# Second layer's attention: softmax inverses spread by transposes of a wide copy, and one near-score product less for block 0

## The reference

```python
for g, (window, dil) in enumerate(((128, 1), (512, 4), (2048, 16))):
    o, l = dilated_prompt(q_p[:, :, g], kv_p[:, :, g, 0], kv_p[:, :, g, 1], window, dil)
    outs_p.append(o)
    lses_p.append(l)
xp = xp + combine_groups(outs_p, lses_p).reshape(b, s, -1) @ w_o_b[j]
```

## Time and profile before

| | |
|---|---|
| median of 3 runs | 1336.86 us (1336.71 to 1337.3) |
| span of the profiled execution | 1336.2 us |
| PE busy | 1256.2 us, 94% |
| DVE busy | 631.5 us, 47% |
| POOL busy | 494.6 us, 37% |
| layer 1's attention (`layer_b`, main loop) | about 648 to 1029 us of the span |
| experts of layer 1 | from about 1061 us to the end |

### The profile page before, as it was taken

One profiled execution on the slowest core, in us unless ns is written; L12 is line 12 of the kernel. 1 busy time (PEld: TensorE's weight loads), 2 busy tenths in 40 slices (PEclk: granted clock), 3 DMA queues, 4 the chain that ended last, 5 costly groups with the idle time before them and its releaser, 6 DMA issues. The chain is left out here.

```text
span 1336.2 us, 21731 instructions
## 1 busy us (share of the span) xinstructions
PE 1256.2 (94%) x8924; PEld 885.1 (66%) x8924; DVE 631.5 (47%) x1023; ACT 399.9 (30%) x839; POOL 494.6 (37%) x415
## 2 busy tenths in 40 slices
PE   8999998999999998889999999999998999998787
PEld 6787887545666655446969868879746656664443
DVE  3578774623722221155357748638546562221114
ACT  2222322402122221255325425426015312221122
POOL 4466655101111111012986676686640101111101
PEclk9999999999999999989999999999999999999999
DMA  8446644477799999981111112013140999999997
GB/s 315 143 143 222 213 126 171 157 308 307 286 418 419 419 417 419 419 349 48 51 57 57 60 57 97 12 57 99 29 123 13 354 375 417 419 419 419 419 419 293
DMA packets 92102, 318.89 MB, mean 239 GB/s; under 512 B 32297, under 2 KB 44729, under 8 KB 65892
## 3 DMA queue, kind: packets, MB, share of 16 engines
q1 hardware_dynamic: 77284, 279.95, 54.1%
q0 software_dynamic: 13536, 33.29, 7.0%
q10 hardware_dynamic: 1184, 4.26, 0.8%
HBM read 300.19 MB, written 33.28 MB: 250 GB/s over the span
## 5 line engine op out<-in xcount | busy, mean ns | idle before, releaser
L1214 PE MATMUL ps<-slots,oT 128*64 128x256 f32 x1216 | 158.9, 392 | 18.5 <-DMA slots<-in_w_up 17.0
L1214 PEld LDWEIGHTS ps<-slots,oT 128*64 128x64 f32 x1216 | 107.8, 141 | 63.5 <-issue 21.6
L1240 DVE TENSOR_TENSOR sg<-sg,ps 64x256 f32<-64x256 f32 x64 | 26.4, 413 | 240.0 <-ACT sg L1237 240.0
L1726 POOL DMA_INDIRECT xs<-xn_rows,idx x30 | 30.8, 1027 | 236.3 <-PE ps L1203 165.9
L2106 PE MATMUL ps<-slots 128*128 128x384 f32 x320 | 107.4, 490 | 1.5 <-DVE vo L2493 1.5
L1237 ACT ACTIVATE sg<-ps 64x256 f32<-64x256 f32 x64 | 24.4, 382 | 234.1 <-PE ps L1214 234.1
L1732 POOL DMA_INDIRECT y_rows<-ysb,idx x30 | 30.2, 1008 | 168.4 <-DVE ysb L1249 168.4
L2106 PEld LDWEIGHTS ps<-slots 128*128 128x128 f32 x320 | 67.3, 215 | 34.7 <-issue 3.8
L1249 DVE COPY ysb<-ps 64x512 f32<-64x512 f32 x60 | 41.6, 694 | 85.8 <-PE ps L1232 81.8
L1232 PE MATMUL ps<-slots,hT 128*64 128x512 f32 x320 | 74.2, 598 | 4.4 <-issue 4.2
L2430 ACT ACTIVATE slots<-slots,neg 128x128 f32<-128x128 f32 (+1 forms) x192 | 64.3, 421 | 43.3 <-DVE neg L2596 43.3
(11 more groups left out here) (374 smaller groups left out, 2636.1 us busy)
## 6 DMA issues: line engine op xcount, KB each, us to landing
slots<-in_w_up SPq DMA_DIRECT2D x42, 1024.0 KB, 29.3
slots<-in_w_down SPq DMA_DIRECT2D x40, 1024.0 KB, 29.0
slots<-in_w_gate SPq DMA_DIRECT2D x34, 1024.0 KB, 29.0
slots<-in_unit_weights_b SPq DMA_DIRECT2D x12, 1536.0 KB, 6.9
wA<-in_qkv_pairs_a SPq DMA_DIRECT2D x24, 512.0 KB, 3.5
apart<-in_w_gate SPq DMA_DIRECT2D x10, 1024.0 KB, 28.5
spare<-in_w_gate SPq DMA_DIRECT2D x8, 1024.0 KB, 12.3
scratch<-in_w_gate SPq DMA_DIRECT2D x8, 1024.0 KB, 20.0
```

The source lines that it names most:

```text
L1214: last = nc.tensor.matmul(bank(q)[lo:lo + CAP, 0:FE], x[:, k, :], wt[:, k, :], start=(k == 0), stop=(k == KT - 1))
```

## The change

It has two parts.

1. `invert` writes the inverses out on DVE into a new SBUF tile `shares` (128 partitions, 4 blocks by 2 heads by 64 equal values, 512 elements) after the reciprocal, and PE's `spread_inverse` is 4 transposes of 128x128 in place of 8 matmuls. DVE waits for its own reciprocal, and, ahead of the reciprocal, for the spread before.
2. For block 0 of the near group the product with the missing block before it is left out: `scores` of half 0 has one product fewer per head (128 columns), the mask pass is 2x384 elements in place of 2x512, the unused quarter of the score tile is set once to -1e30 by a memset, and the mask table is 640 columns in place of 1024.

```diff
-                      ("m0", 4 * 256), ("m1", 128), ("m2", 128)):
+                      ("m0", 128 + 2 * 256), ("m1", 128), ("m2", 128)):
...
+                shares = sb("shares", [128, 4, 2, HD], to=ph)
...
                         elif half == 0:
-                            for kb in range(2):
-                                for h in range(2):
-                                    product(h, 0, 0, 128 * kb, 128)
+                            for h in range(2):
+                                product(h, 0, 0, 128, 128)
                             for h in range(2):
                                 last = product(h, 1, 0, 256, 256)
...
                         for b in range(4):
-                            for h in range(2):
-                                last = nc.tensor.matmul(bank(3)[64 * h:64 * h + 64, 128 * b:128 * b + 128],
-                                                        inverse[:, pair, b, h:h + 1].to_broadcast([128, HD]), ident, start=True, stop=True)
+                            last = nc.tensor.transpose(bank(3)[:, 128 * b:128 * b + 128], shares[:, b].rearrange("p h e -> p (h e)"), ident)
                         last.then_inc(s_ib, 1)
...
-            V.scalar_tensor_tensor(out=dst.rearrange("p h b k -> p h (b k)"), in0=bank(4, 2).rearrange("p (h x) -> p h x", h=2),
-                                   scalar=SCALE, in1=mask("m0")[:, 512 * half:512 * half + 512].unsqueeze(1).to_broadcast([128, 2, 512]),
+            lo = 0 if half else 128
+            V.scalar_tensor_tensor(out=dst.rearrange("p h b k -> p h (b k)")[:, :, lo:512],
+                                   in0=bank(4, 2).rearrange("p (h x) -> p h x", h=2)[:, :, lo:512], scalar=SCALE,
+                                   in1=mask("m0")[:, 128 * half:128 * half + 512 - lo].unsqueeze(1).to_broadcast([128, 2, 512 - lo]),
...
                         dve_do(V.reduce_sum(inverse[:, pair], total[:, pair].rearrange("p i b h -> p b h i"), AX_X))
-                        V.reciprocal(inverse[:, pair], inverse[:, pair]).then_inc(s_inv, 1)
+                        if 2 * j + pair:
+                            dve.wait_ge(s_ib, 2 * j + pair)
+                        dve_do(V.reciprocal(inverse[:, pair], inverse[:, pair]))
+                        V.tensor_copy(shares.rearrange("p b h e -> p (b h) e"),
+                                      inverse[:, pair].rearrange("p b h -> p (b h)").unsqueeze(2).to_broadcast([128, 8, HD])).then_inc(s_inv, 1)
...
                     dve_do(V.memset(tok[:, :, 4, :], 0.0))
+                    dve_do(V.memset(sc[0][:, :, 0, 0:128], NEG))
```

More of the change, by code:

```diff
@@ L87, in constants @@
     put("sid", np.concatenate([token, token + TOK], 1) - NOROW)
[L88 to L93, removed]
+    own, past = np.where(m <= p, 0, NEG), np.where(m >= p, 0, NEG)
+    put("m0", np.concatenate([own, past, own, past, own], 1))
     put("m1", np.where(m <= p, 0, NEG))
```

## The result

The changed kernel takes 1341.08 us (median of 13 runs), the kernel before 1336.24 (13 runs on the same chip). The ratio is 1.0040, 95% interval 1.0030 to 1.0049: 5.3 us slower, between 4.0 and 6.5 (the means lie 5.3 apart, the medians 4.8). The forecast was 2.8 slower, 1339.7, and the range ended at 1341.3.

What follows compares the result with a forecast made beforehand. PE and DVE were both taken to be at their limit at pair 0's spread, so DVE delays there count in full. +6.6 + 0.1 - 0.1 - 1.6 - 2.2 = +2.8 us on 1336.86 gave 1339.7; range 1334.3 to 1341.3.

Steps and rivals of the forecast that it cites:

- the copy of pair 0: DVE copy after the reciprocal, j = 0 to 2: held by POOL's square, 2.2 us late each time, +6.6 us.
- -1.6: Pair 1's spread on PE in j = 0, 1, 2: transposes save 0.53 us each, 3 x 0.53 us gained.
- -2.2: Product left out of `scores` of half 0: 0.27 us saved in each of 8 steps, on PE or the mask pass.
- The last spread: PE's 1.17 us wait for the reciprocal grows about 0.45 by the copy, transposes give back 0.53: -0.1 us.
- sum of +2.8: Total of all terms over the changed loop: +6.6 + 0.1 - 0.1 - 1.6 - 2.2 us, 0.21% slower.
- rival D: Stalls cost more than themselves: PE idles some 3 us per j, clock or POOL/DVE order suffers; 1342.7 us, chance 0.05.
- from 1000 to 1030 PE idled 3.4 us and the clock stayed 1.00: Profile row around the attention's end, cited as evidence that PE's new stalls would not lower the clock.
- one microsecond per stall: Extra cost assumed for each of PE's stalls in j = 0, 1, 2 if the clock or order suffers, giving 1342.7 us.
- I carry each shift of the attention's end to the end of the program one to one: Behind the attention: experts' weights load only once it ends, so the rest moves as a block.
- +0.1: Pair 0's copy in j = 3, free at +0.46 us on DVE, mostly taken up by PE's earlier transposes.
- B: Rival: pair 0's copy is not held, costing +1.4 (0.42 us) to +2.1 (0.7 us); 1334.5 to 1335.5 us, chance 0.16.
- C: Rival: DVE has hidden room before `p_copy(j, 7)`, PE alone sets the pace; -6.4 us, 1330.5 us, chance 0.07.

Runs made afterwards that it cites:

- r5: Changed kernel with pair 0 spread by the old matmuls without copy, pair 1 still by copy and transposes: 1331.88 us, 0.9970 of the kernel before.
- r6: Changed kernel with the copy to `shares` replaced by a reduction over an axis of length one: 1338.07 us, 1.0009 of the kernel before.
- r7: Changed kernel with POOL's square made to wait until pair 0's copy is done: 1335.72 us, 0.9988 of the kernel before.
- r2: Kernel before with only the second part of the change (product left out, shorter mask pass, narrow table), old spread: 1332.55 us, 0.9969 of before.
- r1_again: The changed kernel measured again with no edit: 1342.06 us, 1.0044 of the kernel before.
- r8: Changed kernel with unread filler products in PE's waits in the stages of j = 0 to 2: 1342.30 us, 1.0041 of the kernel before.
- r9: Changed kernel with unread filler products in the stages of j = 0 to 2 and ahead of the last spread: 1338.71 us, 1.0015 of before.
- r12: Repeat of the changed kernel with pair 0 on the old matmuls and only pair 1 on copy and transposes: 1334.73 us, 0.9982 of before.
- r10_again: The changed kernel measured once more with no edit, sent last: 1342.74 us, 1.0043 of the kernel before.
- r11: Changed kernel with two unread filler products only ahead of the last spread: 1343.57 us, 1.0048 of the kernel before.
- r3: Changed kernel with the near product made again and the full mask pass, so only the new spread and narrow table remain: 1345.84 us, 1.0060 of before.

## Why the prediction was right and wrong

**What was right.** The direction, which stood on one step: the copy of pair 0 is held until 0.3 us behind POOL's square and delays `weigh(j, 7)` in full, three times. It was 2.15 us long where 2.2 was said, ended 0.29 behind the square, and was shown from three sides: against the change's 381.54, the loop is 6.85 shorter without the copy (r5), 3.80 with a reduction (r6) and 5.26 with POOL's square behind the copy (r7). The other terms fit too: -1.6 and -2.2 were -3.81 together in r5 and -2.0 for the second in r2. The last spread waited 1.62 instead of 1.17, as worked out. All in all the loop's sum of +2.8 stands against +3.04.

**What was wrong.** The step that failed is the argument against rival D: "from 1000 to 1030 PE idled 3.4 us and the clock stayed 1.00". I set the stalls' own cost at nothing on that row and gave D a chance of 0.05. D came in its form "a clock below 1.00 in the loop": 1.6 us are lost behind the first stage in r1_again, the clock falls there in four further profiles with the same stages, and it does not in r8 and r9, which fill the waits. D's price of 1342.7 lies 1.6 above the measured median; its "one microsecond per stall" was wrong in kind, since one stage of three loses 1.6 and the others nothing.

The row did not bear the argument, because it was one execution. Its idle time was not spread thinly: 1.17 us ahead of the last spread and 1.28 ahead of the next instruction are 2.45 us within 3.5 (1026.83 less 1.17, to 1029.20), closer together than the new waits, 2.59 us within 5.0 (737.19 less 0.73, to 741.46). In the kernel before, full clock came behind them:

```profile
1029.20 3.67 PE L301 MATMUL ps<-slots,oT 128*128 128x512 f32 x8 [1.28 <-PEq L1922]
```

But r5 and r12, one and the same kernel with the same waits in this place, gave 3.67 and 6.64. Whether the clock gives way behind such waits can differ from one execution to the next, and one profile at 1.00 does not price them.

A second step failed beside it: "I carry each shift of the attention's end to the end of the program one to one". The loop of the change is some 4.6 longer than before's in r1_again and r10_again, and the times are 5.9 and 5.7 longer. Over the experiments the time moved from 2.1 less (r2) to 2.5 more (r8) than the loop. So of the 2.5 us by which the forecast was short, 1.6 stand in the loop as the clock's drop (in five of six profiles with these waits), 0.2 as terms of the sum that were off, and the rest lies behind the loop, where no run here fixes the cause.

A smaller term was left out as well. In j = 3 I looked at the spread and not at the copy in front of `weigh(3, 7)`; its new wait of 0.60 lies on the path to the end. The forecast had +0.1 for this place, so it was too low, by no more than the 0.24 us that the loop's sum was short in all.

**What stays open.** Why the clock gave way behind the first of three equal stages and not the others, and why not in the first profile; no run varied the moment at which the waits come. How much of the 2 us behind the loop belongs to the change: where the eight took 3.67 the remainder was 304.5 to 307.0 (five profiles of before, the change, r2, r5, r9) and in r11 312.4; where the eight took longer it was 306.7 to 310.6 (eight profiles). The means are 306.6 with r11, 305.4 without, and 308.4: a difference of 2 or 3 us goes with the eight, and a single profile tells little. I also don't know why r9 gained where r8 and r11 did not; the stages' fill and the last one's were never separated by enough runs.

**The rivals.** B, the copy is not held: wrong for the copy. r6 shows that it holds for a reduction of 0.69 us, B's upper end, but not at B's price: the loop is at -0.76, where B had -1.4 for that length, and the time did not fall. C, PE alone sets the pace: wrong, r3's loop was 7 us longer.

## What to carry to other kernels

Before an operation is put on DVE ahead of something that PE waits for, look what POOL does at that moment: a copy in SBUF of 0.43 us became 2.15 beside a two-input POOL operation, and a reduction that computes the same stayed at 0.69. Where one part of a change costs and another gains, measure the parts alone: here the product left out was as fast by itself (r2) as with the spread of pair 1 beside it. And do not price a new wait of TensorE at nothing on one profile at full clock: profile more than once, since the first profile here was the fastest of 13 runs and the same waits had either level of the clock behind them, and try filler products only as a test of the cause.

## What the runs showed of the hardware that was not expected

- Idle times of 0.73, 0.37 and 1.49 us within 5.0 us were followed by the lower clock level for about 3.5 us in five of the six profiles that had them unfilled, each time only behind the first of three such groups. One idle time of 1.27 or 1.01 us in the same place (r6, r7) was not followed by it, three times in each profile. Idle times of 1.63 and 1.27 us ahead of the output projection had either level behind them, in two profiles of one kernel (r5, r12).
- A DVE copy of 512 elements ran at 0.43 us beside a POOL operation of 4.36 us on 25 elements per partition, and took 2.15 us beside one of 1600 elements. POOL being busy is not by itself what blocks.
- A reduction over an axis of length one copies 512 elements in 0.69 us with POOL's square running beside it.
- Four 128-column transposes took 0.50 us to the next start, and eight matmuls with 64 columns of weights, for the same result, 0.97; replacing the one by the other where PE had no wait (r5) left the clock of the loop at 1.00 in that profile.
